# Sums of the output products on GpSimd, states' products in rounds of row strips, and moved steps in the mixing stage

## What is computed

```python
h = RMSNorm(x); P = h @ W_in                    # conv GLU | z | xBC | dt | gates
# branch a: u = GLU(P); causal depthwise conv of width 31; LayerNorm; silu; @ w_pw
# branch b: causal conv of width 4 on xBC, silu; then per head, with decay from dt:
#   state h_t = exp(dt_t A) h_{t-1} + dt_t x_t B_t^T,  y_t = h_t C_t
#   g = y * silu(z); g = g * rsqrt(mean(g*g) + eps) per group; @ w_ssm_out
x = x + (sigmoid(g_a) * y_a + sigmoid(g_b) * y_b) @ W_out
```

## Time and profile before

| | |
|---|---|
| median of 3 runs | 1857.89 us |
| lowest, highest | 1857.85, 1858.5 us |
| the profiled execution's own time | 1861.42 us |
| its span, first to last instruction | 1859.6 us |
| mean granted TensorE clock | 0.981 of 2.4 GHz |

### The profile page before, as it was taken

The page is one execution under the profiler, slowest core; times in us unless marked ns, Lnnn a source line. Parts: engine busy times, 40 slices in busy tenths (PEclk is TensorE's granted clock), DMA queues, the critical chain, the costliest instruction groups (busy, mean ns, idle before and its releaser), DMA issues.

```text
span 1859.6 us, 28933 instructions
## 1 busy us (share of the span) xinstructions
PE 1770.9 (95%) x11823; PEld 1712.9 (92%) x11823; DVE 1305.7 (70%) x1626; ACT 870.1 (47%) x1473; POOL 95.4 (5%) x149
## 2 busy tenths in 40 slices
PE   7999999999899999998999899998999999999996
PEld 7999999999888898898889888998999999999995
DVE  6963873776739789879887998775556854863764
ACT  5431441444767357726754773255234432441432
POOL 0000000000011101010201100010000000000000
PEclk9999999999989999999999999999999999999998
DMA  4222212214142344153325423232222212222212
GB/s 157 82 73 84 91 69 91 91 62 142 53 141 77 117 121 137 50 163 100 102 74 148 113 70 125 76 131 68 69 76 73 81 67 91 91 69 91 91 44 81
DMA packets 49714, 173.62 MB, mean 93 GB/s; under 512 B 6800, under 2 KB 6960, under 8 KB 45232
## 3 DMA queue, kind: packets, MB, share of 16 engines
q1 hardware_dynamic: 39024, 137.41, 22.5%
q0 software_dynamic: 10560, 34.38, 6.3%
HBM read 155.56 MB, written 16.20 MB: 92 GB/s over the span
## 4 chain that ended last, share of the span: by engine, by line
PE 78%; DVE 11%; ACT 6%; issue 4%; DMA 1%; ACTq 0%; DVEq 0%; SPq 0%; POOLq 0%
PE ps L1615 48%; PE ps L1676 23%; DVE v L1344 4%; DVE pair L1372 2%; PE ps L1633 2%; DVE w_lo L979 1%; PE ps L1836 1%; ACT w_hi L520 1%; DMA ext_a<-in_halo_a 1%; PE ps L1791 1%; PE ps L1642 1%; ACT acb L802 1%; PE ps L1798 1%; PE ps L1804 1%; PE ps L1825 0%
## 5 line engine op out<-in xcount | busy, mean ns | idle before, releaser
L1615 PE MATMUL ps<-xa_hi,w_hi 128*128 128x320 f32 x1504 | 363.8, 323 | 19.0 <-DVE w_lo L979 11.2
L1615 PE MATMUL ps<-xa_lo,w_hi 128*128 128x320 f32 x1504 | 345.2, 311 | 0.0
L1615 PE MATMUL ps<-xa_hi,w_lo 128*128 128x320 f32 x1504 | 345.2, 311 | 0.0
L520 ACT CAST w_hi<-w_raw 128x1024 fp32r<-128x1024 f32 (+2 forms) x188 | 178.7, 951 | 277.1 <-PE ps L1615 240.2
L1676 PE MATMUL ps<-t_hi,w_hi 128*128 128x320 f32 x952 | 297.0, 312 | 11.5 <-issue 11.5
L1615 PEld LDWEIGHTS ps<-xa_hi,w_hi 128*128 128x128 f32 x1504 | 254.0, 190 | 46.8 <-issue 27.9
L1676 PE MATMUL ps<-t_lo,w_hi 128*128 128x320 f32 x952 | 296.4, 311 | 0.0
L1676 PE MATMUL ps<-t_hi,w_lo 128*128 128x320 f32 x952 | 296.2, 311 | 0.0
L979 DVE TENSOR_TENSOR w_lo<-w_raw,w_hi 128x1024 fp32r<-128x1024 f32 (+2 forms) x188 | 208.2, 1108 | 88.6 <-ACT w_hi L520 86.7
L1615 PEld LDWEIGHTS ps<-xa_lo,w_hi 128*128 128x128 f32 x1504 | 254.1, 190 | 0.0
L1615 PEld LDWEIGHTS ps<-xa_hi,w_lo 128*128 128x128 f32 x1504 | 253.9, 190 | 0.0
(11 more groups left out here) (264 smaller groups left out, 2619.9 us busy)
## 6 DMA issues: line engine op xcount, KB each, us to landing
w_raw<-in_w_mix SPq DMA_DIRECT2D x56, 512.0 KB, 3.8
raw_b<-in_w_sp SPq DMA_DIRECT2D x18, 1024.0 KB, 4.8
w_raw<-in_w_sp SPq DMA_DIRECT2D x16, 1024.0 KB, 4.8
w_raw<-in_w_down SPq DMA_DIRECT2D x32, 512.0 KB, 3.7
w_raw<-in_w_tail SPq DMA_DIRECT2D x32, 512.0 KB, 3.7
w_raw<-in_w_gu SPq DMA_DIRECT2D x20, 512.0 KB, 3.8
acb<-cum_dram POOLq DMA_DIRECT2D x20, 512.0 KB, 7.3
w_raw<-in_w_ssm SPq DMA_DIRECT2D x32, 256.0 KB, 2.7
```

The lines of the kernel that those rows point to most:

```text
L520: nc.scalar.copy(hi, w_raw[:, b, 0:width]).then_inc(hi_done, 1)
L1615: last = nc.tensor.matmul(psj[:, b, u, 0:TH], w[:, cols], act_in[:, k, u * TH:(u + 1) * TH], start=(k == 0 and n == 0), stop=(k == chunks ...
```

## The change

In words:

- the sums into `yb` in groups 1 to 3 leave DVE and go to GpSimd (`add_yb`), each after the store of a new state; DVE waits for the sum of two jobs before when it writes `y` again, and `stored` waits for all eight sums.
- the products of the samples' states come in three rounds (`ROUNDS`) of 2, 4 and 2, at the start of job 13, after job 14 and after job 17. Each uses only the 32 token rows that hold its sample. Four banks take part: `pc`, `pd`, `pa`, `pb`.
- long taps of the first GLU chunk: 11 instead of 17 beside the z jobs, none in job 14 and two instead of one in each other output job, then 3 and 2 instead of 4 and 1 in the next group's first jobs. The second chunk has 5, 4, 4, 5, 7, 5 instead of 4, 4, 4, 5, 7, 6.
- on ACT, groups 1 to 3: `long_conv_in(1)` moves behind the cast for job 3; the scales and the decays of tile 0 move to the end of the fifth xBC job, ahead of the cast for job 6; `inverse_root` moves ahead of the cast for job 15, in all groups.
- on DVE the split for job 16 moves right behind the evacuation of job 14.
- in group 0 ACT's steps of dt come behind the evacuation of each job, DVE's addition of dt_bias ahead of the first convolution, and the cumulative sums on PE behind job 5.

The diff, cut to its core:

```diff
--- before.py
+++ after.py
@@ -35,10 +35,13 @@
-TAPS = ({8.5: 5, 9.5: 4, 10.5: 4, 11.5: 4} | {k: 1 for k in range(J_O, GJ)} | {GJ: 4, GJ + 1: 1},
-        {GJ + 2: 4, GJ + 3: 4, GJ + 4: 4, GJ + 5: 5, GJ + 6: 7, GJ + 7.5: 6})
+TAPS = ({8.5: 4, 9.5: 3, 10.5: 2, 11.5: 2} | {k: 2 for k in range(J_O + 1, GJ)} | {GJ: 3, GJ + 1: 2},
+        {GJ + 2: 5, GJ + 3: 4, GJ + 4: 4, GJ + 5: 5, GJ + 6: 7, GJ + 7.5: 5})
+ROUNDS = ((0, 2), (1, 3, 4, 6), (5, 7))
+ORDER = sum(ROUNDS, ())
@@ -200,6 +203,10 @@
+        def state_bank(i):
+            return (pc, pd, pa, pb, pc, pd, pa, pb)[i]
@@ -482,13 +489,23 @@
-                for b in range(NB):
-                    wait(hs_new, NB * g + b + 3)
+                def add_yb(c):
+                    wait(evac_done[c % 2], MIX_HALF + g * (GJ // 2) + (J_O + c) // 2 + 2)
+                    nc.gpsimd.tensor_tensor(yb[:, c], yb[:, c], y[:, c % 2], ALU.add).then_inc(yb_ready, 1)
+
+                for i, b in enumerate(ORDER):
+                    wait(hs_new, NB * g + i + 3)
                     pool.dma_start(d["new_h_sample"][g, b], new_h[b]).then_inc(hs_out[min(b, 1)], 16)
+                    if i and g:
+                        add_yb(i - 1)
+                if g:
+                    add_yb(KM - 1)
...
+                if g:
+                    wait(yb_ready, KM * g)
                 pool.sem_inc(stored, 1)
@@ -714,7 +731,7 @@
-                if k == 5:
+                if k == NX:
                     act.wait_ge(cum_mm, 1)
@@ -832,6 +849,12 @@
+                def scales():
+                    nc.scalar.copy(tokg[:].rearrange("p a t h -> p (a t) h"),
...
+                    act.wait_ge(tokg_ready, g + 1)
@@ -840,8 +863,8 @@
-                    if dt_stage:
-                        dt_stage(k)
+                    if k == 2 and g:
+                        long_conv_in(1, g - 1)
                     xbc_in(k)
@@ -849,23 +872,24 @@
                     if k >= 3:
                         skip(k - 2)
-                    if k == 1 and g:
-                        long_conv_in(1, g - 1)
+                    if dt_stage:
+                        dt_stage(k)
+                    elif k == NX - 2:
+                        scales()
+                        decay(0)
+                        decay_h(0)
...
-                decay(0)
-                decay_h(0)
+                if dt_stage:
+                    decay(0)
+                    decay_h(0)
@@ -899,8 +923,8 @@
                 next_hi(J_U1 + 1)
+                inverse_root(N_GROUP + g, 2 + g)
                 next_hi(J_O)
-                inverse_root(N_GROUP + g, 2 + g)
                 next_hi(J_O + 1)
@@ -1439,25 +1463,28 @@
-                def sample_state(b):
-                    m = NB * g + b
+                def sample_state(i):
+                    b = ORDER[i]
...
-                    dve.wait_ge(hs_mm, m + 1)
-                    nc.vector.tensor_tensor(new_h[b], new_h[b], (pc, pd)[b % 2][:], ALU.add).then_inc(hs_new, 1)
+                    dve.wait_ge(hs_mm, NB * g + next(e for e in (2, 6, 8) if e > i))
+                    nc.vector.tensor_tensor(new_h[b], new_h[b], state_bank(i), ALU.add).then_inc(hs_new, 1)
...
-                    if k > 3 or carried:
+                    if (k > 3 or carried) and k != J_O + 1:
                         split_lo(*at(k + 1), KM * P if k + 1 < J_O or k + 1 == GJ else GC * P)
...
-                    else:
+                    elif k != 2:
                         dt_stage(k)
+                    if not carried and k == 0:
+                        dt_stage(2)
@@ -1506,15 +1533,19 @@
                         if carried:
+                            if c >= 2:
+                                dve.wait_ge(yb_ready, KM * (g - 1) + c - 1)
                             nc.vector.tensor_tensor(halved(y[:, c % 2]), job_out(b), halved(rstd[:]),
                                                     ALU.mult).then_inc(evac_done[b], 1)
-                            evacuated(k)
-                            nc.vector.tensor_tensor(yb[:, c], yb[:, c], y[:, c % 2], ALU.add).then_inc(yb_ready, 1)
+                            if c == 0:
+                                split_lo(*at(k + 2), GC * P)
                         else:
...
+                            if c == 0:
+                                split_lo(*at(k + 2), GC * P)
-                        if c < NB - 2:
-                            sample_state(c + 2)
+                        if 1 <= c < NB - 1:
+                            sample_state(c + 1)
@@ -1826,14 +1857,22 @@
-                def sample(b):
-
-                    if b == 0:
+                def sample_round(r):
+                    first = sum(len(samples) for samples in ROUNDS[0:r])
+                    if r == 0:
...
-                    pe.wait_ge(hs_new, NB * g + b + 1)
-                    nc.tensor.matmul((pc, pd)[b % 2][:], b_one[b], xtl[:], start=True, stop=True).then_inc(hs_mm, 1)
+                    elif r == 1:
+                        pe.wait_ge(var_ready, g + 3)
+                        pe.wait_ge(hs_new, NB * g + 4)
+                    else:
+                        pe.wait_ge(hs_new, NB * g + 6)
+                    for i, b in enumerate(ROUNDS[r]):
+                        rows = slice(b // 2 * 2 * TS, (b // 2 + 1) * 2 * TS)
+                        nc.tensor.matmul(state_bank(first + i)[:], b_one[b][rows], xtl[rows], start=True,
+                                         stop=True).then_inc(hs_mm, 1)
@@ -1849,16 +1888,16 @@
-                            if i in (0, 3):
-                                sample(i // 3)
+                            if i == 0:
+                                sample_round(0)
...
-                        if k - J_O < NB - 2:
-                            sample(k - J_O + 2)
+                        if k in (J_O, J_O + 3):
+                            sample_round(1 + (k - J_O) // 3)
@@ -1871,7 +1910,7 @@
-                        if k == 5 and first:
+                        if k == NX and first:
                             cumulate()
```

More of the change, by code:

```diff
@@ L832, in btok_out @@
                     nc.scalar.copy(btok[:], pb[:, 0:NS]).then_inc(btok_ready, 1)
+                def scales():
+                    nc.scalar.copy(tokg[:].rearrange("p a t h -> p (a t) h"),
+                                   tok[:].rearrange("p a t h -> p (a t) h")[:, :, bass.ds(g * HG, HG)]
+                                   ).then_inc(tokg_ready, 1)
+                    act.wait_ge(tokg_ready, g + 1)
                 if not dt_stage:
@@ L857, in group @@
                     dt_stage(NX)
-                nc.scalar.copy(tokg[:].rearrange("p a t h -> p (a t) h"),
-                               tok[:].rearrange("p a t h -> p (a t) h")[:, :, bass.ds(g * HG, HG)]
-                               ).then_inc(tokg_ready, 1)
-                act.wait_ge(tokg_ready, g + 1)
-                if dt_stage:
+                    scales()
                     act.wait_ge(cum_out, 16)
```

## The result

The changed kernel takes 1869.52 us (median of 4 runs, 1868.87 to 1870.65) against 1857.87 us of the kernel before on the same chip (4 runs, 1856.28 to 1858.50): ratio 1.0065, 95% interval 1.0051 to 1.0080. It is slower by about 12 us, where 1840 was forecast. The profiled execution has a span of 1868.8 us, 9.2 more than before.

What follows compares the result with a forecast made beforehand. PE, busy 95%, was taken to bound the kernel, DVE second. Group 0 -10.2 and groups 1 to 3 -8.1, plus 0.8 for the clock, gave -17.5: median 1857.89 to 1840 us, range 1829 to 1867.

Steps and rivals of the forecast that it cites:

- GpSimd's sums ... I cost them at nothing: Output jobs, groups 1 to 3: sums of 0.83 to 1.66 us fit in 3.66, off PE's path; cost nothing.
- The third rival: Output jobs, groups 1 to 3: GpSimd's sums block VectorE's two-SBUF-input instructions for their whole length; 1854 to 1868 us, chance 0.38.
- D: Length of one GpSimd sum, 0.83 to 1.66 us; blocking would cost 16.5 D in three groups.
- The point from which it decides: If sums block VectorE, the change becomes a loss when a sum exceeds 17.5/16.5 = 1.06 us.
- The new group: Groups 1 to 3: 113.1 to the last z job plus 53.1, 166.2 us each; -8.1 us over three.
- Rounds: State products in the mixing stage: 1.19 us a round, 3.6 for three against 6.9; 3.3 us less PE work a group.
- the rival had put 8: State products of a round do not overlap, four cost 3.44: some +2 us a group, 1848 us, chance 0.10.
- Output jobs: Groups 1 to 3: DVE needs 3.66 us a job against PE's 3.52; +1.0 us over seven jobs.
- Early decays: Decays ahead of job 6's cast, groups 1 to 3: DVE stalls 4.0, PE about 4.2; tile 0 3.3 us later.
- The rival of free decays: Groups 1 to 3: the stall of 4.0 us from the early decays shrinks; 1828 us, chance 0.10.
- Turn 2: Tiles, groups 1 to 3: waits 1.87 at 898.67 before the change; forecast at 901.2 in the third group.
- Group 0: PE stands 4.7 us after 503.25, tile 0 at 538.2 (-8.0), output stage gains 2.2; -10.2 us in all.

Runs made afterwards that it cites:

- sums_left_out: Changed kernel without GpSimd's 24 output sums, all waits and orders kept: 1843.86 us, 0.9932 of the kernel before.
- one_input_copy: Changed kernel with GpSimd copying y into the output tile in place of each sum: 1854.22 us, 0.9981 of the kernel before.
- best_at_split_one_tap: Changed kernel, GpSimd's sums held until VectorE's next split, tile 0's decays in groups 1 to 3 and the tap table as before the change: 1823.37 us.
- at_split_decays_back: Changed kernel, GpSimd's sums held until VectorE's next split, scales and decays of tile 0 in groups 1 to 3 back in their old place: 1831.53 us.
- full_rows: `at_split_decays_back` with the state products in the same rounds but each over all 128 rows instead of 32: 1844.63 us.

## Why the prediction was wrong

- **The failed step** is "GpSimd's sums ... I cost them at nothing". It was the one term whose cover was VectorE's not being slowed, and it cost 26 us (`sums_left_out`). The third rival was the case, in its place, its mechanism and its price. The rival had put the sum about 1.2 us after the state's sum, in the second tap, which is what the timeline shows, and with D = 1.66 it gave 1868; a sum takes 1.58 and holds VectorE up for 1.73, and the kernel took 1869.5, just above the range's end of 1867. Its chance was too small: 0.38 against 0.42 for the forecast. The trace of before had no instruction of GpSimd that reads SBUF beside a tap; DMA issues that leave a tap at 0.88 were no evidence on sums, and the Trainium skill's rule, which the rival names, stood against the forecast.
- **The point from which it decides**, D of 1.06 us, was right in kind: the copy with its 0.84 us in each pair of taps gives 1854, a gain of 0.2%.
- **All the other terms together**: without the sums the changed kernel takes 1843.9 against 1840 forecast, and with them placed at the split 1845.8. The new group was put at 166.2 us; `sums_left_out` has 165.5.
- **Rounds**: 1.19 us was taken for each, 1.13 is measured, and serial products cost 13 us more, where the rival had put 8. Right.
- **Output jobs**: 3.66 us with VectorE as the bound was forecast; in group 2 of `sums_left_out` two of the seven steps between evacuations are 3.65, and the others 1.74, 3.96, 4.77, 3.96 and 4.19. Together they are 25.9 us against 7 times 3.66 = 25.6, so the sum was right and the even pace was not: the longest step has a round of two in it.
- **Early decays**: the stall of VectorE was put at 4.0 us and PE's at about 4.2; measured 3.94 and 4.06, 4.35 at most. Tile 0 was put at 66.8 us after the group's start and comes at 66.9. The forecast had tile 0 3.3 us later by the move, and the rival priced the stall at 12 us in three groups. Taking the move out gains 14.3 us, or 10.7 with one tap in each output job, so it was a loss as forecast. The rival of free decays falls. Turn 2 was put at 85.0 us after the group's start and comes there, and the wait that was to move from job 3 to job 4 does so: it is 1.87 at 843.74. VectorE's stall in group 2 of the changed kernel:

```profile
861.16 1.22 DVE L1003 TENSOR_TENSOR w_lo<-w_raw,w_hi 128x1024 fp32r<-128x1024 f32 x1 [3.94 <-ACT w_hi L537]
```

- **Group 0**: job 5 was to wait 4.7 us and waits 4.14. Tile 0 was to come at 538.2, 8.0 us earlier, and comes at 539.36 after another wait of 3.57. This execution began the block 1.3 us earlier (486.05 for 487.34), so from the block's start the tile comes only 5.6 us earlier. The group was to give 10.2 us and gave 8.3; in the seven experiments with the same group 0 it gave 8.9 to 9.6. Right in kind, too large by 0.6 to 1.9. The rows of PE:

```profile
506.51 0.90 PE L1646 MATMUL ps<-xa_hi,w_hi 128*128 128x320 f32 x2 [4.14 <-DVE w_lo L1003]
539.36 1.68 PE L1822 MATMUL ps<-mdec,xdt 128*64 128x128 f32 x16 [3.57 <-issue]
```

- **After group 3** nothing was to change; 2.7 us were lost there in the profiled execution (707.7 for 705.0). The sums don't explain it: `sums_left_out` takes 707.2 there without any, and `one_input_copy` 705.7. The cause stays open.

## What to carry to other kernels

Work that is moved from VectorE to GpSimd isn't off the path if it reads SBUF while VectorE, being the bound, runs an instruction with two SBUF inputs: count its whole length on VectorE there. Tie its start to the VectorE instruction behind which the PSUM reads come, by a semaphore that exists already: the same 24 sums cost 26 us in one place and about 2 us in another, where the one compared above starts 1.8 us later after its evacuation. And when one change takes work off the bounding engine, ask what the engine that was second now has for slack: the sums on GpSimd were a gain of 0.2% while VectorE had 1.34 to 1.37 us to spare in four of the seven steps, and a loss when it had none.

## What the runs showed of the hardware

- A sum of two tiles of 128x640 fp32 takes 1.58 us on GpSimd and 0.83 on VectorE, 1.9 times; a copy of one such tile takes 0.73 on GpSimd and a memset 0.65. The ratio is close to that of the Trainium skill ("GPSIMD Engine Reference", section "3.1 Elementwise — side-by-side cycle accounting": 1.96, at 2048 elements).
- The sum held VectorE up for more than the part that overlapped: a tap begun at 956.88 ended at 959.48, 0.7 us after a sum of 957.22 to 958.79, and two taps took 1.73 us more for a sum of 1.58. I had not expected an instruction whose record has begun to be overtaken.
- It also goes the other way. The last sum of each group starts 0.25 us into the first tap of a pair, which keeps its 0.87 us, and takes 2.05 us itself. The row of GpSimd, of the changed kernel:

```profile
988.14 2.05 POOL L494 TENSOR_TENSOR yb<-yb,y 128x640 f32<-128x640 f32 x1 [2.74 <-DVE y L1538]
```

  Which of the two is held was not settled, and the starts in the records don't tell it: second taps of a pair that began 0.34 us before a sum were held in the changed kernel, and a single tap that began 0.36 us before one was not (931.06 and 931.42 in `best_at_split_one_tap`; the sum took 1.95).
- Four fp32 products of 32 rows each, in four row strips and four PSUM banks, take 1.13 us together, as long as two of them (944.51 in `at_split_decays_back`). Over 128 rows one costs 0.86 us, and four take 3.60 (`full_rows`).
